# Windowed attention in a diffusion trunk: key parts stacked on the contraction, value heads on column halves, the sink as a score column, probabilities scaled on GpSimd

## The reference: what is computed

```python
def sink_attend(q, keys, vals, sink, mask):
    logits = jnp.einsum('bqgrd,bkgd->bgrqk', q, keys) * (AT_HD ** -0.5)
    logits = jnp.where(mask, logits, -jnp.inf)
    s = sink[None, :, :, None]
    m = jnp.maximum(jnp.max(logits, axis=-1), s)
    p = jnp.exp(logits - m[..., None])
    denom = jnp.sum(p, axis=-1) + jnp.exp(s - m)
    return jnp.einsum('bgrqk,bkgd->bqgrd', p / denom[..., None], vals)
```

## Time and profile before

| | |
|---|---|
| median of three runs | 2097.64 us |
| profiled execution | 2097.79 us, span 2096.0 us |
| PE busy | 1961.0 us, 94% of the span |
| DVE / ACT / POOL busy | 1192.7 / 690.3 / 22.4 us |
| attention, first pass, first rotation to last output copy | 1336.3 to 1469.6 us |
| attention, second pass | 1484.4 to 1626.4 us |
| mean granted TensorE clock | 0.967 |

### The profile page before, as it was taken

The page is one execution under the profiler, slowest core; times in us unless marked ns, Lnnn a source line. Parts: engine busy times, 40 slices in busy tenths (PEclk is TensorE's granted clock), DMA queues, the critical chain, the costliest instruction groups (busy, mean ns, idle before and its releaser), DMA issues.

```text
span 2096.0 us, 25879 instructions
## 1 busy us (share of the span) xinstructions
PE 1961.0 (94%) x10776; PEld 1640.8 (78%) x10776; DVE 1192.7 (57%) x2032; ACT 690.3 (33%) x1049; POOL 22.4 (1%) x18
## 2 busy tenths in 40 slices
PE   4999999999889899999999998899899889999997
PEld 2999999999878688888888887665665767777875
DVE  2555556555764666336542664755454478477485
ACT  3333333333222333113321332355154334133232
POOL 0000000000300000000000000000000000000000
PEclk9999999999999899999999999889989999999998
DMA  6221222112202133323332322100100212232332
GB/s 268 91 78 44 81 81 81 61 61 81 71 1 61 51 121 111 100 93 119 121 101 93 109 91 94 51 11 1 51 10 1 79 62 91 81 99 81 91 93 98
DMA packets 45333, 165.82 MB, mean 79 GB/s; under 512 B 4897, under 2 KB 5281, under 8 KB 45089
## 3 DMA queue, kind: packets, MB, share of 16 engines
q1 hardware_dynamic: 45216, 164.16, 23.7%
HBM read 162.05 MB, written 2.10 MB: 78 GB/s over the span
## 4 chain that ended last, share of the span: by engine, by line
PE 78%; DVE 14%; ACT 4%; DMA 2%; issue 2%; SPq 0%; DVEq 0%
PE slot L375 20%; PE slot L377 19%; PE slot L376 19%; DVE ACC L1375 6%; PE MA L510 4%; PE slot L704 3%; DVE WL L1059 3%; PE MB L428 3%; PE slot L695 2%; ACT WH L769 1%; DMA WR<-in_w 1%; PE MB L461 1%; PE MB L421 1%; DVE ACC L1383 1%; DMA ada_raw<-in_ada 1%
## 5 line engine op out<-in xcount | busy, mean ns | idle before, releaser
L375 PE MATMUL slot<-HH,WH 128*128 128x256 f32 (+2 forms) x2016 | 726.3, 360 | 44.5 <-DVE HL L1157 16.9
L376 PE MATMUL slot<-HL,WH 128*128 128x256 f32 (+2 forms) x2016 | 708.7, 352 | 0.0
L377 PE MATMUL slot<-HH,WL 128*128 128x256 f32 (+2 forms) x2016 | 708.3, 351 | 0.0
L375 PEld LDWEIGHTS slot<-HH,WH 128*128 128x128 f32 x2016 | 384.9, 191 | 125.4 <-issue 76.8
L376 PEld LDWEIGHTS slot<-HL,WH 128*128 128x128 f32 x2016 | 385.1, 191 | 38.1 <-issue 2.2
L377 PEld LDWEIGHTS slot<-HH,WL 128*128 128x128 f32 x2016 | 384.1, 191 | 38.5
L1059 DVE TENSOR_TENSOR WL<-WR,WH 128x1024 fp32r<-128x1024 f32 x204 | 249.3, 1223 | 246.0 <-ACT WH L769 244.4
L769 ACT ACTIVATE WH<-WR 128x1024 fp32r<-128x1024 f32 x204 | 215.4, 1057 | 368.2 <-DMA WR<-in_w 368.1
L1375 DVE SCALAR_TENSOR_TENSOR ACC<-UP,cw,ACC 128x512 f32<-128x512 f32 x352 | 263.9, 750 | 8.6
L375 PE MATMUL slot<-GH,WH 128*128 128x512 f32 (+1 forms) x528 | 192.3, 364 | 8.4 <-DVE GL L1388 8.4
L377 PE MATMUL slot<-GH,WL 128*128 128x512 f32 (+1 forms) x528 | 190.9, 362 | 0.0
(11 more groups left out here) (177 smaller groups left out, 1837.7 us busy)
## 6 DMA issues: line engine op xcount, KB each, us to landing
WR<-in_w SPq DMA_DIRECT2D x204, 512.0 KB, 3.6
ada_raw<-in_ada SPq DMA_DIRECT2D x84, 512.0 KB, 4.6
AD<-in_ada SPq DMA_DIRECT2D x3, 2048.0 KB, 23.2
X<-in_x SPq DMA_DIRECT2D x1, 3072.0 KB, 11.9
out<-Y SPq DMA_DIRECT2D x8, 256.0 KB, 2.2
Y<-in_masks SPq DMA_DIRECT2D x1, 512.0 KB, 19.7
ada_raw<-in_rope SPq DMA_DIRECT2D x1, 512.0 KB, 3.5
small<-in_small SPq DMA_DIRECT2D x1, 327.5 KB, 2.9
```

The source lines that it names most:

```text
L375: mm(SLOT[s][:, po], WH[w % NB][:, k, :], hi[:, k, to], start=(k == 0), stop=False)
L376: mm(SLOT[s][:, po], WH[w % NB][:, k, :], lo[:, k, to], start=False, stop=False)
L377: last = mm(SLOT[s][:, po], WL[w % NB][:, k, :], hi[:, k, to], start=False, stop=(k == kn - 1))
```

## The change

**Operands.** Instead of KH, KO (keys' high and low part, both halves in one tile) there is for each half a tile KS of 128 partitions with the high part on the half's own 64 partitions and the low part on the other 64. QH and QO, one tile for each half, hold the same 64 rows twice. A product QH\*KS then gives high\*high + high\*low at once, and QO\*KS adds low\*high (and low\*low).

**Rope stage.** The high parts are now made on ACT, two copies for each of the key's and context's halves and four for a query tile, in pieces of 64 partitions; ACT waits for DVE's sum (`raw_roped`) and DVE waits for ACT's copies (`hi_copied`) before it subtracts, also in pieces. WL of a weight tile is made before these subtractions.

**Unit loop.** Units now alternate between the halves. Two products for the scores in place of three. The sink is a column of the scores, made by a product of a tile of ones with one column, so maximum, exponential and sum run over one column more and the instructions on es and den go. POOL scales PB. The values are multiplied for every pair of units, 128 columns at a time, alternately to output partitions 0 to 63 and 64 to 127; slot 1 holds two blocks. PT has four buffers of one unit.

```diff
-            KH = sb("KH", [P, TOK], F32R, s)
-            KO = sb("KO", [P, TOK], F32R, s)
-            QH = sb("QH", [P, 4, LAT], F32R, s)
-            QO = sb("QO", [P, 4, LAT], F32R, s)
+            KS = [sb(f"KS{i}", [P, TOK], F32R, s) for i in range(2)]
+            QH = [sb(f"QH{i}", [P, 4, LAT], F32R, s) for i in range(2)]
+            QO = [sb(f"QO{i}", [P, 4, LAT], F32R, s) for i in range(2)]
...
-        UNITS = [(bi, half, r) for bi in range(LAT // P) for half in range(2) for r in range(4)]
+        UNITS = [(bi, half, r) for bi in range(LAT // P) for r in range(4) for half in range(2)]
...
+            for i in range(2):
+                for u in range(len(UNITS)):
+                    n = 2 + window(UNITS[u][0])[1]
+                    pool.wait_ge(rden_ready, i * len(UNITS) + u + 1)
+                    pool.tensor_scalar(PB[u % 3][:, 0:n * P], PB[u % 3][:, 0:n * P], rden[u % 4][:, :], None, ALU.mult).then_inc(probs_scaled, 1)
...
-                parts_of = [(QH, KH), (QH, KO), (QO, KH)]
-                for e, (a, b) in enumerate(parts_of):
-                    mm(S[:, PC0:PL0], a[hp, r, q], b[hp, 0:CTX], start=(e == 0), stop=(e == 2))
+                for e, a in enumerate((QH, QO)):
+                    mm(S[:, PC0:PL0], a[half][:, r, q], KS[half][:, 0:CTX], start=(e == 0), stop=(e == 1))
...
+                end = PL0 + n * P
+                mm(S[:, end:end + 1], ones[:, :].to_broadcast([P, P]), sink8[:, hd], start=True, stop=True).then_inc(at_scores, 1)
...
-                pe.wait_ge(pt_ready, unit.times(1, (4 * v + 4)))
...
+                pe.wait_ge(pt_ready, unit.times(1, (2 * v + 2)))
...
-                    last = mm(SLOT[1][64 * half:64 * half + 64, 0:512], AV[:, c, 64 * half:64 * half + 64],
-                              PT[v % 2][:, j, :, :].rearrange("p r q -> p (r q)"), start=(j == 0), stop=(j == n + 1))
+                    for half in range(2):
+                        last = mm(SLOT[1][64 * half:64 * half + 64, o:o + P], AV[:, c, 64 * half:64 * half + 64],
+                                  PT[(2 * v + half) % 4][:, j * P:(j + 1) * P], start=(j == 0), stop=(j == n + 1))
...
-                at_score(0, *UNITS[0])
                 pe.wait_ge(roped, rot.now())
-                at_score(1, *UNITS[1])
+                at_score(0, i, *UNITS[0])
+                at_score(1, i, *UNITS[1])
...
                     if u + 3 < len(UNITS):
-                        at_score(u + 3, *UNITS[u + 3])
-                    if u % 4 == 0 and u:
-                        at_values(u // 4 - 1, *UNITS[u - 1][:2])
+                        at_score(u + 3, i, *UNITS[u + 3])
                     at_turn(u, *UNITS[u])
+                    if u % 2 == 0 and u:
+                        at_values(u // 2 - 1)
...
+                def query_parts(r):
+                    his.add()
+                    act.wait_ge(raw_roped, his.now())
+                    for half in range(2):
+                        for to in (64 * half, 64 - 64 * half):
+                            last = go(QH[half][to:to + 64, r, :], RAW[(r + 1) % 2][64 * half:64 * half + 64, :], ACT.Copy)
+                    last.then_inc(hi_copied, 1)
...
-                link(tt(RAW[b][:, :], RAW[b][:, :], ROT[:, :], ALU.add))
-                link(cp(hi, RAW[b][:, :]))
-                tt(lo, RAW[b][:, :], hi.bitcast(F32), ALU.subtract).then_inc(roped, 1)
+                tt(RAW[b][:, :], RAW[b][:, :], ROT[:, :], ALU.add).then_inc(raw_roped, 1)
...
                 w = u - 2
                 if w >= 0:
-                    dve.wait_ge(sink_ready, unit.times(1, (w + 1)))
-                    mark(tt(den[w % 4][:, :], den[w % 4][:, :], es[w % 4][:, :], ALU.add))
...
+                    dve.wait_ge(probs_ready, unit.times(1, (w + 1)))
+                    nc.vector.reciprocal(rden[w % 4][:, :], den[w % 4][:, :]).then_inc(rden_ready, 1)
...
                 for r in range(4):
-                    rope_one(QH[:, r, :], QO[:, r, :], (r + 1) % 2)
+                    rope_one((r + 1) % 2)
                     split_low(first + min(r + 4, 7))
+                    dve.wait_ge(hi_copied, rot.now())
+                    for half in range(2):
+                        h = slice(64 * half, 64 * half + 64)
+                        for to in (64 * half, 64 - 64 * half):
+                            last = tt(QO[half][to:to + 64, r, :], RAW[(r + 1) % 2][h, :], QH[half][h, r, :].bitcast(F32), ALU.subtract)
+                    last.then_inc(roped, 1)
```

More of the change, by code:

```diff
@@ L187, in trunk @@
             den = [sb(f"den{i}", [P, 1], F32, s) for i in range(4)]
[L188 to L190 removed]
+            rden = [sb(f"rden{i}", [P, 1], F32, s) for i in range(4)]
         SLOT = [ctx.enter_context(nc.psum_tensor(f"slot{i}", [P, 1024], F32)) for i in range(2)]
@@ L237, in trunk @@
         rope = AR[0]
+        PT = [t[:, :, :].rearrange("p f o -> p (f o)")[:, 0:5 * P] for t in AR[1:4]] + [PX[:, :]]
         BACK, FORE = 0, 1
@@ L1029, in two_key_heads @@
                     if u + 3 < len(UNITS):
-                        at_exp(u + 3, i, *UNITS[u + 3][1:])
+                        at_exp(u + 3)
                 unit.add(len(UNITS))
-                pair.add(8)
+                pair.add(len(UNITS) // 2)
+            his = Tally()
             vals = Tally(HEADS)
@@ L1408, in _ @@
             norm_dve(TOK, norm_g[0][:, 1, :], 48 + SC1 * KC, 48 + SH1 * KC)
-            ts(nsink[:, :], part("sink"), -1.0, None, ALU.mult).then_inc(roped, 2)
+            ts(sink8[:, :], part("sink"), 1.0 / (AT_SCALE * P), None, ALU.mult).then_inc(roped, 2)
             dve.wait_ge(roped, 2)
@@ L1453, in two_key_heads @@
             def two_key_heads(i):
                 first = tile.now()
-                rope_one(KH[:, CTX:TOK], KO[:, CTX:TOK], 0)
-                link(cp(KH[:, 0:CTX], AVT[:, 0:CTX]))
-                mark(tt(KO[:, 0:CTX], AVT[:, 0:CTX], KH[:, 0:CTX].bitcast(F32), ALU.subtract))
+                rope_one(0)
                 split_low(first + 3)
+                dve.wait_ge(hi_copied, rot.now())
+                for half in range(2):
+                    h, o = slice(64 * half, 64 * half + 64), slice(64 - 64 * half, 128 - 64 * half)
+                    tt(KS[half][o, 0:CTX], AVT[h, 0:CTX], KS[half][h, 0:CTX].bitcast(F32), ALU.subtract)
+                    last = tt(KS[half][o, CTX:TOK], RAW[0][h, :], KS[half][h, CTX:TOK].bitcast(F32), ALU.subtract)
@@ L1467, in two_key_heads @@
                 at_evac(3, i)
-                unit.add(32)
-                pair.add(8)
+                unit.add(len(UNITS))
+                pair.add(len(UNITS) // 2)
                 tile.add(6)
```

93 lines of the change are left out of this document (47 added, 46 removed).

## The result

| | before | after |
|---|---|---|
| median | 2099.24 us (2085.96 to 2101.28, 4 runs) | 2131.06 us (2127.15 to 2136.66, 4 runs) |
| profiled execution, span | 2097.79, 2096.0 us | 2127.15, 2125.4 us |
| rope stage, both passes | 67.3 us | 95.5 us |
| unit loops, both passes | 208.1 us | 213.2 us |

A forecast was written before the change was run, and what follows sets the result against it. PE was taken as the bound, busy nearly throughout the rope stage and unit loops. From the profiled 2097.8 us, the loops' 27.7 came off and the rope stage's 20.7 went on: 2090.8, say 2091 us, range 2066 to 2124.

The forecast's parts named there:

- POOL's scaling: Unit loop: POOL's scaling taken at 0.75 us (0.65 in end blocks), bounds 0.69 to 1.28, the low one if DVE doesn't contend.
- POOL over 1 us: Unit loop: one of the listed signs that would show the forecast wrong, a POOL scaling longer than 1 us.
- POOL is the late one: Rival, unit loop: POOL's scaling takes 1.28 us, 0.53 more for some 28 pairs, +15 us, 2106; chance 0.10.
- it stays at half throughout: Rival, unit loops: clock stays at 1.2 GHz now value products are short, +53 us a pass, 2197; chance 0.07.
- Values, columns side by side: Value products: column halves overlap, 0.245 us a chunk of keys; with 0.2 for entering and leaving, 1.43 a middle block.
- halves in turn: Rival, value products: column halves take turns, 0.43 us a chunk in place of 0.245, +27 us, 2118; chance 0.14.
- Scores and sink column: Unit loop on PE: a unit's scores, edges and sink column take 1.0 us, 0.86 in an end block.
- the sink's column takes back what stacking saves: Scores: dropping the third product saves 0.29 us (0.24 in end blocks); the sink's column adds 0.23.
- The loop's sum: Unit loops: pairs of 5.34 and 4.6 us, 90.2 us a pass, 180.4 together, 27.7 less than before.
- the clock's term: Unit loops: 14 us at half speed do the work of about 8 and cost 5.8 us, left as before.
- The rope stage: Rope stage: DVE, ACT, DVE in series, 7.9 us between rotations where PE has 6.35 of work; +20.7 us over both passes.
- is mostly hidden: Rope stage: half clock after the new pauses falls mostly within the same waits; given no separate size.

The follow-up runs named there:

- e5: e1 with GpSimd multiplications by one on scratch tiles added in several forms, at program start and in the first unit loop; ran once, 2087.2 us, read for durations alone.
- e9: The change with POOL's scaling written as two operations (times 1/sum, plus 0) in place of one; 2083.7 us, 0.992 of the kernel before.
- e8: The change with six more unused 128-column products on PE before the transposes of every second unit; 2117.5 us, 1.012 of the kernel before.
- e2: The change with the rope stage and three score products of the kernel before, POOL's scaling kept; 2132.0 us, 1.015 of the kernel before.
- e6: The kernel before with only the scaling of the probabilities moved from DVE to POOL; 2150.6 us, 1.026 of the kernel before.
- e3: The change with DVE scaling and with the rope stage and three score products of the kernel before; 2065.5 us, 0.985 of the kernel before.
- e1: The change with the scaling given back from POOL to DVE, all else as changed; 2073.6 us, 0.989 of the kernel before.
- e12: e7 without the sink in the softmax at all; 2042.2 us, 0.973 of the kernel before.
- e7: e1 with a shorter rope stage: two query low-part subtractions, not four, other half zeroed once, shorter DVE wait, WL last; 2049.9 us, 0.977 of before.

## Why the prediction was wrong, step by step

- **POOL's scaling, the step that failed.** The prediction took 0.75 and 0.65 us, bounds 0.69 to 1.28, from the earlier trace rows. Measured 1.89 and 1.57. The rows were of an instruction with two operations and the change issues one with one (e5). The bounds were meant to hold both ends and held only one form; I had read engine, operation and columns, and left out the second operation in the code. The prediction's own sign of being wrong, POOL over 1 us, came true. e9 puts it right by the form alone: 2083.7, within the range and 7 us from the forecast. The choice of the low bound, that DVE does not slow POOL in this loop, was right: 0.70 us in e9 for 512 columns, 0.69 on scratch tiles at the program's start (e5). The rival "POOL is the late one" named the mechanism and priced it with the same bound, at 2106. In all the loops came out 32.8 us over the forecast and the rope stage 7.5.
- **The clock.** The prediction left it as before in the loop and carried the rival that it stays at half throughout. It did neither: 0.86, falling after pauses. e8 shows that it cost at least 15 us; the sum had no term that tied the clock to a wait that the change brings. With POOL's size it is what makes the difference of 47: 28.5 us of waits and 17.0 of longer records. The rival's reading that full clock came back only with long value products does not hold either: in the change it was 1.00 from 1384.2 to 1387.4, before the first value product at 1391.35. What sets the size of this term stays open (e2, e6).
- **Values, columns side by side.** Right: 0.21 us a chunk (taken 0.245), with the entering 1.24 us a block against 1.43. The rival of halves in turn falls.
- **Scores and sink column.** Right in size: 1.02 us a unit against 1.0. That the sink's column takes back what stacking saves is borne out in part: 7.1 us a pass saved (e3 against e1), 2.6 to 3.8 a pass that the column counts (e12). As the rope stage costs more than that, stacking as written loses (e3 is 8 us faster than e1), and as in e7 it gains.
- **The loop's sum.** 180.4 us forecast; 167.6 in e9, where the scaling took the forecast's time. So the rest of the loop was counted 13 us too long. The eight pairs of the middle blocks take 40.4 us a pass, not 42.7: in the pair shown above PE's turn with values is shorter by 0.2 and the wait on POOL 0.58 in place of 0.7. The rest lies in the end blocks, the start and end of a pass and the clock's term of 5.8 us a pass, and is not taken apart.
- **The rope stage.** Mechanism right, size too small: +28.2 in place of +20.7. The middle intervals are 3.19 to the first copy, 2.59 to the first subtraction, 2.78 and 0.15 = 8.71, forecast 7.9. The terms mis-sized are the copies (0.64 each, taken 0.53) and the subtractions (0.70, taken 0.61): the earlier trace rows gave the spacing of instructions of 128 partitions in a stream. Single instructions take as long for 64 partitions as for 128 (copies 0.63 and 0.61, subtractions 0.69 and 0.68), but in the earlier trace rows each starts before the last has ended, and here not. Why not is open. The last interval was 11.8, forecast 10.3, with 1.0 of the difference the rotation at half clock. That half clock behind the pauses "is mostly hidden" was wrong for this one. In e9 the errors of -12.8 and +7.7 nearly cancel, so its closeness to 2091 is in part luck.

## What to carry to other kernels

Before an instruction's price is taken from a row, compare the code of both lines down to the number of operations and the kind of scalar: engine, name and shape in the trace are not the whole form. When work moves to an engine that stood idle, its own duration enters a chain (here maximum, reciprocal, scaling, transposes) and a pause on TensorE can be paid a second time through the clock; here the relief would have paid only if the engine that gave the work away had been the bound, and DVE was not. When one operand has to be doubled for stacking, count whether the doubled low part is needed at all: zeros, written once, did the same for half the subtractions.

## What the runs showed of the hardware

- A GpSimd multiplication with one operation took 1.49 us for 512 fp32 columns, with two operations (times, plus 0) 0.62; with the scalar from SBUF 0.07 more. Slopes 2.5 and 0.82 ns a column. DVE took 0.49 for 512 with the scalar from SBUF.
- Work with no use made the program faster: six products in each of 15 waits a pass raised the granted clock of the loops from 0.86 to 0.93 and 0.95 (e8) and took 7.6 us off each.
- The sum of TensorE's pauses does not tell the granted clock: 50 us idle in two loops with 0.86 (the change), 27 with 0.76 (e6), 21 with 0.90 and 0.96 (e9), 13 with 0.96 and 0.93 (e1).
- Two column halves of 64 with 128 columns each start in pairs some 0.11 us apart, the two of a pair 0.007 apart, 20 records in 1.31 us: side by side.
- ACT and DVE instructions on 64 partitions take as long as on 128: for 512 columns 0.63 and 0.61 us (ACT, copy), 0.69 and 0.68 (DVE, subtraction). Four in a row start 0.64 and 0.70 apart, where eight of 128 partitions start 0.53 and 0.61 apart.
